# Axial attention as one run of 32 interleaved units, with the next queries and a projection inside it

## The chip, the cores and the metric

The kernel runs on one core of a Trainium2 chip. The metric is the device time of one execution in microseconds (us), from its first to its last instruction and what lies around it. The median of three runs before the change is 3224.26 us (3221.07 to 3228.34).

## What is computed

A sequence of 512 tokens of width 1024 goes through two transformer blocks of a first kind (each once) and two layers of a second kind. Only the second kind is touched. In float32:

```python
def second_block(x, ...):
    for l in range(2):
        h = rmsnorm_2(x, norm_mix_pre[l])
        qa, ka, va, pu, qc, kc, vc, gl = split(h @ w_in[l])
        ya = global_axial_attention(qa, ka, va, qk_norm_q[l], qk_norm_k[l])
        yb = pool_mixer(pu, w_pool[l], pool_scale[l])
        yc = neighbourhood_attention(qc, kc, vc, rpb[l])
        merged = sum(sigmoid(gates) * branches(ya, yb, yc))
        x = x + rmsnorm_2(merged @ w_out[l], norm_mix_post[l])
        h = rmsnorm_2(x, norm_ffn_pre[l])
        x = x + rmsnorm_2(conv_gated_mlp(h, ...), norm_ffn_post[l])

def global_axial_attention(q, k, v, gq, gk):
    # 8 query heads, 2 key/value heads, head width 64, no mask
    q = rope_2d(rmsnorm(q, gq), row, col) * 64 ** -0.5
    k = rope_2d(rmsnorm(k, gk), row, col)
    o = softmax(q @ k.T) @ v
```

The neighbourhood attention has eight heads with keys and values of their own and a bias and a mask for each pair of tokens.

## The kernel before, in words

Activations lie transposed, channels on partitions. A projection multiplies split operands: each weight tile and each activation has a high and a low part, and `three` (L470 to L472) issues three matmuls for each of the eight 128-channel steps k. One such step is called a part below. Weights come in entries: SyncE loads an entry into `raw` (L339), GpSimd splits it into `wh` and `wl` (L449 to L452) once TensorE is through with the buffer, and TensorE waits for `w_split`. There are two buffers, used in turn.

An attention works in units: one head and one tile of 128 queries against all 512 keys. TensorE computes the scores into bank S0 or S1, VectorE scales or biases them and takes the row's minimum (`score`, L1400 in the axial stage, L1404 elsewhere; scores are kept negated), ScalarE takes the exponential and its sum (`soften`, L1106), TensorE transposes the result with four matmuls (`transposed`, L621), ScalarE copies it from PSUM (`copy_turned`, L1112), and TensorE multiplies by the values. These steps of different units overlap: in slot t TensorE issues the scores of unit t, the transposes of unit t - 2 and the weighted matmuls of unit t - 3. Every engine runs its instructions in the order written and waits on counting semaphores.

The **axial stage** of a layer (`axial` in each engine's block, `attend` and `units`) has four groups of eight units, each with two query heads, one for each key head. Groups 0 to 2 are the iterations of a loop, group 3 stands behind it. The probabilities are stationary in the weighted matmuls and the values move, 64 columns (`weighted`, L627). VectorE scales each unit's output into `y_tok` (L1433); at a group's end four matmuls transpose it (L615), ScalarE and VectorE split it into `yh` and `yl` (L1117, L1415). Into slots 0 to 2 of a group go the eight parts of the next group's query projection (`AHEAD`, `q_part`, result in bank PA). Its result is scaled (`scale_q`, L1589) and squared (`q_square`, L1165), copied with a gain (L1170), summed by head on TensorE (`q_sum`, L774), rooted on ScalarE (`q_root`, L1178, a function of another table than the exponential) and rotated: TensorE permutes the channels (`turn_rotate`, L782), VectorE multiplies by cosine (`q_cosine`, L1574) and sine and adds (`turn`, L1579, L1582). `TURN` gives the slots; the sine product waits until slot 9, since the turned queries overwrite `q_sb`, which the group's own scores still read.

Behind the stage TensorE runs the neighbourhood's first query and key projection (`qk_part(H("na_q0", l), 0, 2 * DT)`, 16 parts) and its value projection (`v_projection`, L566 to L568).

The **neighbourhood stage** (`attention` with kind "na") is one unrolled run of 32 units. Even slots issue two score matmuls, on partitions 0 to 63 and 64 to 127 (L683). The values are stationary, 64 columns, and the transposed probabilities move, so the two heads of a pair write the two halves of one bank (`weighted_pair`, L722). The softmax's division is done once for a group: TensorE spreads the reciprocals over a bank (`den_turn`, L737), ScalarE copies them (L1157), VectorE multiplies (`y_divide`, L1454). `FILL` says how many parts of the next group's projections go into each of a group's eight slots, `last_plan` those of the last twelve slots, `Y_TURN` where the divisions stand. The other attentions of the kernel use the same function.

## Time and profile before

| | |
|---|---|
| median of three runs | 3224.26 us |
| the profiled execution's own time | 3222.63 us |
| its span, first to last instruction | 3220.5 us |
| mean granted TensorE clock | 0.98 of 2.4 GHz |
| TensorE busy | 3101.5 us |
| GpSimd, VectorE, ScalarE busy | 1661.9, 1420.2, 796.3 us |

The profile is one execution on the chip. PE is TensorE's matmuls, PEld its weight loads, DVE is VectorE, ACT ScalarE, POOL GpSimd, SP SyncE. L470 is line 470 of the kernel. In a list of instructions in order of time (the timeline), a line has the start in us from the span's start, the duration, the engine, line, operation, out<-in, the number of records merged, and in brackets the engine's idle time before it and what ended it. Float32 matmuls leave two records each. Matmuls are pipelined, so their durations overlap; the steps from start to start are what they cost. A line of windows has the stretch in us from the span's start, its length, the busy time and (x) the instructions of PE, PEld, DVE, ACT and POOL, the mean granted clock (PEclk), the DMA engines' busy share and GB/s.

### The profile page before, as it was taken

The page shows a single profiled execution, that of the slowest core. Times are in us where ns is not written, and L with a number is a line of the kernel's source. Part 1 is how long each engine was busy: PE and PEld are TensorE (multiplying, and loading weights), DVE is VectorE, ACT ScalarE, POOL GpSimd, SP SyncE. Part 2 cuts the span into 40 slices and gives each one's busy share as a digit, 9 for nine tenths or more (in the row PEclk, how much of TensorE's full clock was granted, in tenths as well). Part 3 has the DMA queues.
Part 4 walks back from the last instruction along what each step waited for, and adds up shares of the span by engine and source line. Part 5 has one row for each costly group of instructions (what it writes and reads, how often), then busy time and mean ns, then how long its engine had stood idle before and what let it go on. Part 6 is the DMA issues. An engine that isn't in the chain of part 4 may idle for free.

```text
span 3220.5 us, 45047 instructions
## 1 busy us (share of the span) xinstructions
PE 3101.5 (96%) x14716; PEld 2438.9 (76%) x14716; DVE 1420.2 (44%) x2535; ACT 796.3 (25%) x1441; POOL 1661.9 (52%) x1254
## 2 busy tenths in 40 slices
PE   8998999999799999899999999999899999999998
PEld 6776888886578888667678878888667678878886
DVE  3244444223444431542533476631633434476622
ACT  2333221113322210243421122210242411132201
POOL 4334666663156667312346656676312356656674
PEclk9999999999999999999999999999899999999999
DMA  6251223322022233101412222232112322222232
GB/s 159 74 167 63 96 93 104 107 95 66 27 79 97 93 109 105 52 26 51 101 59 98 90 74 98 95 110 95 40 33 56 83 79 97 86 72 98 98 107 83
DMA packets 99595, 274.79 MB, mean 85 GB/s; under 512 B 38126, under 2 KB 38894, under 8 KB 99490
## 3 DMA queue, kind: packets, MB, share of 16 engines
q1 hardware_dynamic: 97328, 269.07, 25.9%
q10 hardware_dynamic: 2162, 4.36, 0.7%
q8 instruction: 61, 1.00, 0.1%
q14 instruction: 44, 0.36, 0.0%
HBM read 269.66 MB, written 11.54 MB: 87 GB/s over the span
## 4 chain that ended last, share of the span: by engine, by line
PE 71%; DVE 3%; issue 2%; ACT 1%; DVEq 0%; ACTq 0%
PE PA L470 11%; PE PA L471 10%; PE PA L472 10%; PE PB L470 8%; PE PB L471 8%; PE PB L472 8%; PE T L621 2%; PE O L627 2%; PE S L590 2%; PE O L722 1%; PE S L683 1%; PE O L502 1%; DVE strip L1756 0%; DVE tmps L1365 0%; DVE hl L1326 0%
## 5 line engine op out<-in xcount | busy, mean ns | idle before, releaser
L452 POOL TENSOR_TENSOR wl<-raw,wh 128x1024 fp32r<-128x1024 f32 (+2 forms) x416 | 1129.2, 2714 | 33.3
L449 POOL TENSOR_TENSOR zero<-zero 128x1 f32<-128x1 f32 x416 | 82.4, 198 | 1494.0 <-PE PA L472 786.9
L470 PE MATMUL PA<-hh,wh 128*128 128x512 f32 x1392 | 563.5, 405 | 27.9 <-DVE hl L1326 8.3
L471 PE MATMUL PA<-hl,wh 128*128 128x512 f32 x1392 | 548.9, 394 | 0.0
L472 PE MATMUL PA<-hh,wl 128*128 128x512 f32 x1392 | 548.4, 394 | 0.0
L450 POOL CAST wh<-raw 128x1024 fp32r<-128x1024 f32 (+2 forms) x416 | 476.3, 1145 | 0.0
L470 PEld LDWEIGHTS PA<-hh,wh 128*128 128x128 f32 x1392 | 265.4, 191 | 136.4 <-issue 66.0
L470 PE MATMUL PB<-hh,wh 128*128 128x512 f32 x896 | 357.1, 399 | 0.0
L472 PE MATMUL PB<-hh,wl 128*128 128x512 f32 x896 | 349.3, 390 | 0.0
L471 PE MATMUL PB<-hl,wh 128*128 128x512 f32 x896 | 349.1, 390 | 0.0
L472 PEld LDWEIGHTS PA<-hh,wl 128*128 128x128 f32 x1392 | 265.4, 191 | 57.4
L471 PEld LDWEIGHTS PA<-hl,wh 128*128 128x128 f32 x1392 | 265.2, 191 | 53.0 <-issue 1.6
L1106 ACT ACTIVATE probs<-biased,stats 128x512 f32<-128x512 f32 (+2 forms) x240 | 155.2, 647 | 406.7 <-PE T L621 222.0
L1685 DVE SCALAR_TENSOR_TENSOR tmps<-S,cols,tmps 128x511 f32<-128x511 f32 (+1 forms) x264 | 197.9, 750 | 39.6 <-DVE tmps L1685 19.8
L470 PEld LDWEIGHTS PB<-hh,wh 128*128 128x128 f32 x896 | 168.2, 188 | 47.5 <-issue 14.4
L472 PEld LDWEIGHTS PB<-hh,wl 128*128 128x128 f32 x896 | 168.1, 188 | 35.6
L471 PEld LDWEIGHTS PB<-hl,wh 128*128 128x128 f32 x896 | 168.6, 188 | 33.8 <-issue 1.2
L621 PEld LDWEIGHTS T<-ident,probs 128*128 128x128 f32 x792 | 98.0, 147 | 72.0 <-issue 36.8
L1202 ACT ACTIVATE T<-tmps 128x512 f32<-128x512 f32 x88 | 53.0, 602 | 391.9 <-DVE tmps L1685 391.9
L470 PE MATMUL PA<-acth,wh 128*128 128x512 f32 x352 | 137.4, 390 | 0.0
L471 PE MATMUL PA<-actl,wh 128*128 128x512 f32 x352 | 137.0, 389 | 0.0
L472 PE MATMUL PA<-acth,wl 128*128 128x512 f32 x352 | 136.9, 389 | 0.0
(298 smaller groups left out, 4865.6 us busy)
## 6 DMA issues: line engine op xcount, KB each, us to landing
raw<-in_w_up SPq DMA_DIRECT2D x176, 512.0 KB, 3.4
raw<-in_w_down SPq DMA_DIRECT2D x64, 768.0 KB, 4.2
raw<-in_w_merge SPq DMA_DIRECT2D x48, 768.0 KB, 4.1
raw<-in_w_out SPq DMA_DIRECT2D x32, 512.0 KB, 3.4
strips_na<-in_rpb SPq DMA_DIRECT2D x1, 7620.0 KB, 31.7
raw<-in_w_pool SPq DMA_DIRECT2D x12, 512.0 KB, 3.4
raw<-in_w_na_qk SPq DMA_DIRECT2D x12, 512.0 KB, 3.4
raw<-in_w_na_v SPq DMA_DIRECT2D x8, 512.0 KB, 3.4
```

Source lines behind the costliest of these rows:

```text
L449: nc.gpsimd.tensor_tensor(zero[:, :], zero[:, :], zero[:, :], ALU.add)
L450: nc.gpsimd.tensor_copy(wh[s][:, 0:width], raw[s][:, 0:width]).then_inc(w_head, 1)
L452: nc.gpsimd.tensor_tensor(wl[s][:, 0:width], raw[s][:, 0:width], wh[s][:, 0:width].bitcast(F), ALU.subtract).then_inc(w_split, 1)
L470: mm(dst, h_, rh, start=first, stop=False)
L471: mm(dst, h_, rl, start=False, stop=False)
L472: return mm(dst, l_, rh, start=False, stop=last)
L590: mm(SB[t % 2][:, 0:L], q_sb[r, qt * P:qt * P + P], k_sb[r, 0:L], start=True, stop=True).then_inc(s_ready, 1)
L621: last = nc.tensor.transpose(TB[t % 2][:, k * P:k * P + P], probs[t % 2][:, k * P:k * P + P], ident[:, :])
L627: last = mm(OB[t % 2][:, 0:dv], probsT[t % 2][:, k * P:k * P + P], values(k), start=(k == 0), stop=(k == L // P - 1))
L1106: A(probs[t % 2][:, 0:L], biased[t % 2][:, 0:L], ACT.Exp, scale=-1.0, bias=mn[:, t % 8:t % 8 + 1], accum_out=den[:, t % 8:t % 8 + 1]).then ...
L1202: A(GELU[:, :], tmp[0][:, :], f).then_inc(gelu_ready, 1)
L1685: ins = STT(out=dst[:, lo:hi], in0=src[:, lo - d:hi - d], scalar=w(k), in1=dst[:, lo:hi], op0=ALU.mult, op1=ALU.add)
```

## The change

The axial stage becomes a third kind of `attention`, unrolled over 32 units in the neighbourhood's form: scores in pairs, values stationary, division once a group at slots 11, 19, 27 and 35. Keys lie in `kr_sb`, values in `tmp[4]`; the queries of successive groups alternate between `q_sb` and `qr_sb`. The next queries' projection parts keep slots 0 to 2 of a group. The whole turn now lies within the group: scaled in slot 3, squared in 4, the sums and the permutation on TensorE in slot 5 (`q_turn`, the permutation into PA instead of PB), the sine product in place in PSUM and the sum in slot 6 (`q_turned`), the root on ScalarE in slot 6, its reciprocal in slot 7. The 16 parts of the neighbourhood's first projection move from behind the stage into slots 24 to 34.

```diff
-        c.update(a=3, b=8, u=32, g=4, d=4 * (UNIT_LINKS[kind] + TURN_LINKS), r=4)
+        c.update(a=3, b=2 + 3, u=32, g=4, d=TURN_LINKS + UNIT_LINKS[kind], r=4, dr=16, dc=4)
...
-UNIT_LINKS = {"causal": 0, "na": 2, "diff": 8 + 4 + 1 + 3, "axial": 8, "mla": 4 + 1}
+UNIT_LINKS = {"causal": 0, "na": 2, "diff": 8 + 4 + 1 + 3, "axial": 3 * 3, "mla": 4 + 1}
...
-AHEAD = {"axial": [3, 3, 2, 0, 0, 0, 0, 0, 0, 0, 0, 0]}
...
-FILL = [3, 3, 2, 2, 3, 3, 0, 0]
+FILL = {"moba": [3, 3, 2, 2, 3, 3, 0, 0], "axial": [3, 3, 2, 0, 0, 0, 0, 0]}
+FILL["diff"] = FILL["dil"] = FILL["na"] = FILL["moba"]
 Q_AT, K_AT = 3, 6
 Y_TURN = {"moba": (15, 23, 27, 35), "diff": (15, 23, 30, 38)}
+Y_TURN["axial"] = (11, 19, 27, 35)
...
-TURN = dict(scale=3, square=4, sum=5, root=5, cosine=6, rotate=7, turn=9)
+TURN = dict(scale=3, square=4, sum=5, cosine=5, turn=6, root=6, invert=7)
...
+def axial_turn(b, n):
+
+    return {**b, "e": b["e"] + 2 * (n - 1), "a": b["a"] + n - 1, "b": b["b"] + 2 + n - 1, "r": b["r"] + n, "turn": n}
...
-        rq = stats[:, 108:116]
+        rq_of = stats[:, 108:116], stats[:, 88:96]
...
+        turned_q, axial_key, axial_v = strip[0][:, 0:S], kr_sb, tmp[4]
...
                 pe.wait_ge(s_taken, b["u"] + 2)
                 pe.wait_ge(pt_copied, b["u"] + 2)
...
                 def part(j):
+                    if j == 0 and after_turns is not None:
+                        pe.wait_ge(ax_done, after_turns)
                     if j == DT:
...
-                full = kind == "na"
+                full = kind in ("na", "axial")
+                values = (lambda g, c, k: axial_v[:, k * P + c:k * P + c + 64]) if kind == "axial" else (
+                    lambda g, c, k: V[:, k, g * P + c:g * P + c + 64])
...
-                parts = sum((qk_parts({**b, **{n: b[n] + m * g for n, m in (("e", 2), ("a", 1), ("b", 1))}},
-                                      *((y_split, 2 * (b["g"] + max(g - 1, 0)) + 1) if kind == "diff" else
-                                        (den_copied, b["dc"] + max(g - 1, 0))))
-                             for g in range(3)), []) + list(last_parts)
-                slots = FILL * 3 + list(last_plan)
+                if kind == "axial":
+                    parts = sum((q_parts(axial_turn(b, n)) for n in (1, 2, 3)), []) + list(last_parts)
+                else:
+                    parts = sum((qk_parts({**b, **{n: b[n] + m * g for n, m in (("e", 2), ("a", 1), ("b", 1))}},
+                                          *((y_split, 2 * (b["g"] + max(g - 1, 0)) + 1) if kind == "diff" else
+                                            (den_copied, b["dc"] + max(g - 1, 0))))
+                                 for g in range(3)), []) + list(last_parts)
+                slots = FILL[kind] * 3 + list(last_plan)
                 slots += [0] * (end + 1 - len(slots))
                 assert sum(slots) == len(parts)
...
                 def score(t):
                     g, head, qt = t // 8, t % 2, t // 2 % 4
-                    if t == 0:
+                    if kind == "axial":
+                        if t % 8 == 0:
+                            pe.wait_ge(ax_done, b["r"] + g + 1)
+                    elif t == 0:
                         pe.wait_ge(pa_taken, b0["a"] + 2)
                         pe.wait_ge(pb_taken, b0["b"] + 2)
                     elif t % 8 == 0:
...
-                    mm(SB[head][:, 0:span(t)], queries[g % 2][r, qt * P:qt * P + P], keys[g % 2][r, 0:span(t)],
+                    mm(SB[head][:, 0:span(t)], queries[g % 2][r, qt * P:qt * P + P],
+                       (axial_key if kind == "axial" else keys[g % 2])[r, 0:span(t)],
                        start=True, stop=True).then_inc(s_ready, 1)
...
                     if t in turns:
-                        (y_turn if kind == "diff" else den_turn)(b, turns.index(t))
+                        (y_turn if kind == "diff" else den_turn)(b, turns.index(t), kind)
+                    if kind == "axial" and t < 24 and t % 8 == TURN["sum"]:
+                        q_turn(axial_turn(b, t // 8 + 1))
                     for part in parts[sum(slots[:t]):sum(slots[:t + 1])]:
                         part()
...
-                            weighted_pair(OB[g % 2], tv // 2 % 4, span(tv), g)
-
-            def weighted_pair(bank, qt, L, g):
+                            weighted_pair(OB[g % 2], tv // 2 % 4, span(tv), lambda head, k: values(g, 64 * head, k))
+
+            def weighted_pair(bank, qt, L, values):
...
-                        c = g * P + head * 64
-                        last = mm(bank[r, q], V[:, k, c:c + 64], probsT[head][:, k * P:k * P + P], start=(k == 0),
+                        last = mm(bank[r, q], values(head, k), probsT[head][:, k * P:k * P + P], start=(k == 0),
                                   stop=(k == L // P - 1))
...
-                if g < 3:
+                if g < 3 and kind == "axial":
+                    pe.wait_ge(pb_taken, b["b"] + 2 + min(g + 1, 3) + 1)
...
+            def q_parts(b):
+
+                def part(k):
+                    if k == 0:
+                        pe.wait_ge(ax_done, b["r"])
+                    q_part(b, k, k + 1)
+
+                return [lambda k=k: part(k) for k in range(DT)]
+
+            def q_turn(b):
+
+                pe.wait_ge(den_copied, b["dc"] + b["turn"] - 1)
+                q_sum(b["b"], b["r"])
+                pe.wait_ge(ax_n, b["r"] + 1)
+                mm(PA[:, :], perm[1][:, :], turned_q, start=True, stop=True).then_inc(ax_rot, 1)
+
...
-                def group(i, ahead):
-                    bi = step(b, i, **STEP["axial"])
-                    pe.wait_ge(ax_done, bi["r"] + 1)
-
-                    attend(bi, 8, "axial", lambda h, k: tmp[4][:, k * P + h * 64:k * P + h * 64 + 64], 64,
-                           ahead=step(b, i + 1, **STEP["axial"]) if ahead else None, plan=AHEAD["axial"])
-
-                with pe.Fori(0, 3) as i:
-                    group(i, True)
-                group(3, False)
+                mm(PB[:, :], perm[1][:, :], src, start=True, stop=True).then_inc(ax_rot, 1)
...
-                axial_kv(H("axial_kv", l)); pool_tiles(H("pool", l), H("axial_kv", l), H("axial", l)); axial(H("axial", l))
-                qk_part(H("na_q0", l), 0, 2 * DT)
-                v_projection(H("na_v", l), True)
+                axial_kv(H("axial_kv", l)); pool_tiles(H("pool", l), H("axial_kv", l), H("axial", l));
+                q0 = H("na_q0", l)
+                attention(H("axial", l), None, "axial", qk_parts(q0, den_copied, q0["dc"] - 1, after_turns=q0["r"]),
+                          [2, 2, 2, 1, 1, 0, 0, 2, 2, 2, 2])
+                v_projection(H("na_v", l))
...
+                    if kind == "axial" and t < 24:
+                        bn = axial_turn(b, t // 8 + 1)
+                        if t % 8 == TURN["square"]:
+                            q_square(bn["a"] + 2, gain)
+                        if t % 8 == TURN["root"]:
+                            q_root(bn["r"])
...
-                A(qr_sb[:, :], tmp[2][:, :], ACT.Copy, scale=gain).then_inc(ax_n, 1)
+                A(turned_q, tmp[2][:, :], ACT.Copy, scale=gain).then_inc(ax_n, 1)
...
-                    at = 2 * (t % 4) + t // 4
-                    TS(biased[t % 2][:, 0:L], SB[t % 2][:, 0:L], rq[:, at:at + 1], None, ALU.mult, ALU.min,
+                    rq = rq_of[t // 8 % 2]
+                    TS(biased[t % 2][:, 0:L], SB[t % 2][:, 0:L], rq[:, c:c + 1], None, ALU.mult, ALU.min,
...
-                        c = 0 if dv == P else 64 * (tv // 4)
-                        TS(y_tok[0][:, tv % 4, c:c + dv], OB[tv % 2][:, 0:dv], rden[:, tv:tv + 1], None,
-                           ALU.mult).then_inc(o_taken, 1)
-                    if ahead is not None:
-                        if t == TURN["scale"]:
-                            scale_q(ahead)
-                        elif t == TURN["cosine"]:
-                            q_cosine(ahead["r"])
-                        elif t == TURN["turn"]:
-                            link(v.reciprocal(rq, rq_root))
-                            turn(-0.125, ahead["b"], ahead["r"], q_sb[:, :])
...
+                chain_at(b["d"] + (TURN_LINKS if kind == "axial" else 0))
+                if kind == "na":
...
+                    if kind == "axial" and t < 24:
+                        bn = axial_turn(b, g + 1)
+                        if t % 8 == TURN["scale"]:
+                            scale_q(bn)
+                        if t % 8 == TURN["cosine"]:
+                            q_cosine(bn["r"])
+                        if t % 8 == TURN["turn"]:
+                            q_turned(bn)
+                        if t % 8 == TURN["invert"]:
+                            dve.wait_ge(pb_taken, bn["b"] + 2)
+                            link(v.reciprocal(rq_of[(g + 1) % 2], rq_root))
+                    elif t < 24 and t % 8 == Q_AT:
                         take_q(ahead(g), g + 1)
-                    if t < 24 and t % 8 == K_AT:
+                    if kind != "axial" and t < 24 and t % 8 == K_AT:
                         take_k(ahead(g), g + 1)
...
+            def q_turned(b):
+
+                dve.wait_ge(ax_rot, b["r"] + 1)
+                link(STT(out=PA[:, :], in0=PA[:, :], scalar=-0.125, in1=rope[:, 1, :], op0=ALU.mult, op1=ALU.mult))
+                TT(queries[b["turn"] % 2][:, :], tmp[0][:, :], PA[:, :], ALU.add).then_inc(ax_done, 1)
...
-                axial(H("axial", l), l)
-                q0 = H("na_q0", l)
-                dve.wait_ge(s_ready, q0["u"] + 1)
-                take_q(q0, 0); take_k(q0, 0); v_copy(H("na_v", l))
+                attention(H("axial", l), "axial", 0, H("na_q0", l))
+                v_copy(H("na_v", l))
```

## Rows read from the trace of the kernel before

**Rows 1.** The page, busy time of each engine

```profile
PE 3101.5 (96%) x14716; PEld 2438.9 (76%) x14716; DVE 1420.2 (44%) x2535; ACT 796.3 (25%) x1441; POOL 1661.9 (52%) x1254
```

**Rows 2.** Windows, first layer: four axial groups, first projection, neighbourhood stage

```profile
1376.93:1411.24 34.31, 32.98 (x151) 21.65 (x151) 11.62 (x37) 15.88 (x31) 4.03 (x6) 0.86 0.06 16
1411.24:1441.06 29.82, 28.55 (x151) 19.18 (x151) 12.38 (x39) 16.34 (x33) 4.02 (x6) 1.00 0.10 35
1441.06:1476.40 35.34, 34.74 (x152) 23.52 (x151) 12.39 (x39) 16.52 (x33) 7.07 (x6) 0.81 0.09 30
1476.40:1497.63 21.23, 20.43 (x117) 13.57 (x117) 9.66 (x34) 10.96 (x26) 0.00 (x0) 1.00 0.00 1
1497.63:1508.40 10.77, 10.77 (x51) 8.92 (x50) 1.45 (x3) 0.66 (x2) 3.57 (x3) 1.00 0.02 3
1530.47:1631.10 100.63, 99.39 (x693) 69.08 (x692) 47.08 (x135) 46.77 (x103) 29.36 (x22) 1.00 0.32 80
```

**Rows 3.** Windows of the second layer: third axial group; sum of the five stretches

```profile
2396.60:2431.88 35.28, 34.68 (x151) 23.41 (x150) 12.38 (x39) 16.46 (x33) 7.08 (x6) 0.81 0.09 30
...
sum 135.77, PE 132.51 PEld 90.17 DVE 47.51 ACT 60.47 POOL 18.71; mean PE 26.50 PEld 18.03 DVE 9.50 ACT 12.09 POOL 3.74
```

**Rows 4.** Timeline of TensorE, fourth axial group

```profile
1487.71 1.12 PE L590 MATMUL S<-k_sb,q_sb 64*128 64x512 f32 x2
...
1490.19 1.12 PE L590 MATMUL S<-k_sb,q_sb 64*128 64x512 f32 x2
```

**Rows 5.** Timeline of TensorE, neighbourhood stage

```profile
1543.31 0.50 PE L470 MATMUL PB<-hh,wh 128*128 128x512 f32 x1
...
1545.49 0.60 PE L621 MATMUL T<-ident,probs 128*128 128x128 f32 x4
...
1549.76 1.13 PE L683 MATMUL S<-k_sb,q_sb 64*128 64x512 f32 x4
...
1551.40 1.09 PE L722 MATMUL O<-probsT,V 128*64 128x128 f32 x16
1552.43 0.66 PE L621 MATMUL T<-ident,probs 128*128 128x128 f32 x4
1553.02 1.13 PE L683 MATMUL S<-kr_sb,qr_sb 64*128 64x512 f32 x4
...
1576.76 1.05 PE L737 MATMUL PB<-ident,stats 128*64 128x128 f32 x16
1577.73 0.66 PE L621 MATMUL T<-ident,probs 128*128 128x128 f32 x4
```

**Rows 6.** Timeline of GpSimd, a split behind the first projection

```profile
1510.12 2.40 POOL L452 TENSOR_TENSOR wl<-raw,wh 128x1024 fp32r<-128x1024 f32 x1
```

**Rows 7.** Timeline of all engines, the turn of the next queries, first axial group

```profile
1395.10 0.62 ACT L1165 ACTIVATE tmps<-tmps 128x512 f32<-128x512 f32 x1
...
1395.62 0.71 ACT L1170 ACTIVATE qr_sb<-tmps,cols 128x512 f32<-128x512 f32 x1
...
1395.77 1.05 PE L774 MATMUL PB<-onesblk,tmps 128*128 128x2 f32 x8 [0.22 <-ACT tmps L1165]
...
1397.42 0.72 ACT L1106 ACTIVATE probs<-biased,stats 128x512 f32<-128x512 f32 x1 [1.09 <-PE T L621]
...
1398.14 0.58 ACT L1112 ACTIVATE probsT<-T 128x512 f32<-128x512 f32 x1
...
1398.73 1.28 ACT L1178 ACT_TABLE_LOAD   x1
...
1399.25 0.75 DVE L1400 TENSOR_SCALAR_CACHE_REDUCE biased<-S,stats 128x512 f32<-128x512 f32 x1 [2.50 <-PE S L590]
...
1400.03 0.27 ACT L1178 ACTIVATE stats<-PB,eps 128x8 f32<-128x8 f32 x1
```

**Rows 8.** Timeline of TensorE, start of the first axial group

```profile
1376.93 2.06 PE L590 MATMUL S<-k_sb,q_sb 64*128 64x512 f32 x2 [1.76 <-DVE q_sb L1582]
...
1383.01 1.12 PE L590 MATMUL S<-k_sb,q_sb 64*128 64x512 f32 x2
```

More of the change, by code:

```diff
@@ L1178, in q_root @@
                 A(rq_root, PB[:, 0:8], ACT.Sqrt, scale=1.0 / 64, bias=eps[:, 0:1]).then_inc(pb_taken, 1)
-            def axial(b, gain):
-                b = after_first(b)
-                with act.Fori(0, 3) as i:
-                    units({**step(b, i, **STEP["axial"]), "gain": gain}, 8, "axial", i, ahead=step(b, i + 1, **STEP["axial"]))
-                units(step(b, 3, **STEP["axial"]), 8, "axial", 3)
             def mla(b):
@@ L1279, in _ @@
                 q_root(ax["r"])
-                axial(ax, gain)
+                attention(ax, "axial", 0, gain=gain)
                 attention(H("na", l), "na", 8)
@@ L1556, in attention @@
                             in1=yh[:, ytile + g, :].bitcast(F), op0=ALU.mult, op1=ALU.subtract).then_inc(y_split, 2)
-                done(4 * UNIT_LINKS.get(kind, UNIT_LINKS["causal"]))
+                done((1 if kind == "axial" else 4) * UNIT_LINKS.get(kind, UNIT_LINKS["causal"]))
             def done(per):
```

104 lines of the change are left out of this document (33 added, 71 removed).

## The prediction

> **What bounds the kernel now.** I read the page first: TensorE is busy for 3101.5 of the span's 3220.5 us [rows 1], so only what shortens TensorE's own queue, or its few stalls, can move the time. Next I cut the part that the diff touches into windows by group, from a group's first score matmul to the next group's [rows 2, 3]. The reader is to see three things. In the first layer the four axial groups take 34.31, 29.82, 35.34 and 21.23 us and the neighbourhood's first projection behind them 10.77: 131.47 together. In the second layer the same five stretches sum to 135.77. And TensorE is busy in 95% or more of nearly all of them, so the stage is bound by TensorE's instructions, not by waits; the third group is 5.5 us longer than the second for the same work, with a mean granted clock of 0.81 instead of 1.00, that is partly at 1.2 GHz instead of 2.4.
>
> Then the timeline, for what a unit (one head, one query tile) costs. In the axial stage without projection work between, one score matmul, four transposes and four weighted matmuls repeat every 2.48 us (1487.71 to 1490.19) [rows 4]. The neighbourhood stage, which already has the form that the change gives to the axial one, runs a pair of units every 3.26 us (1549.76 to 1553.02), 1.63 a unit [rows 5]. Its two score matmuls, on the upper and lower 64 rows, take 1.13 us together, as one does in the axial stage (1.12), and its weighted matmuls, with values stationary and 64 columns each, 1.03 us for both heads. With 0.59 for a unit's transposes (1552.43 to 1553.02), twice, a score pair's own step is what is left of 3.26, about 1.06. That halving is the gain to expect.
>
> **The change part by part**, per layer, steps taken start to start.
>
> *Units.* 32 units become 16 pairs: 16 x 3.26 = 52.2 us [rows 5].
>
> *Projection parts.* Three parts (nine matmuls) take 1543.31 to 1545.49, 2.18 us, so 0.73 each with the hand-over [rows 5]. The 24 parts for the next queries stay, 16 of the neighbourhood's first projection come in from behind the stage: 40 x 0.73 = 29.2. With those 16 go all that they issue: their two weight entries are loaded and split earlier (the buffers come free at the third group's parts, long before slot 24), and VectorE's two copies of their result sit at slots 29 and 36. These moves cost nothing: in the windows before, GpSimd is busy 4.03 to 7.07 us of 30, VectorE about 12 [rows 2]. If that cover were gone, TensorE would wait for a split at the v projection. That is the one close place: its second entry's buffer comes free in slot 34, a cast and a split end some 3.6 us later (2.40 of it the split [rows 6]), and the projection wants it only after the rest of slot 34, the last turn and its first entry, over 5 us later. SyncE's loads for the neighbourhood's bias strips stand behind these entries and keep their place relative to the v projection.
>
> *Turns.* Dividing a group by its sums is now one matmul group of 1576.76 to 1577.73, 0.97, four times: 3.9 [rows 5]. It replaces four y transposes a group, with their drain at each group's end, and takes the 32 small VectorE scalings away. The query turn keeps its two TensorE steps, the sums (1.05 long, 0.95 step) and a 512-column permutation matmul, which I take as a score, 1.06 [rows 5, 7]: 3 x 2.0 = 6.0.
>
> Work: 52.2 + 29.2 + 3.9 + 6.0 = 91.3.
>
> *Check of this way of adding.* The neighbourhood stage has 16 pairs, 60 parts, four turns: 52.2 + 43.8 + 3.9 = 99.9, against 100.63 measured [rows 2]. So 0.7 is left for start and tail; I add it here too.
>
> *Start.* The first score and three parts run at 1.2 GHz: 1376.93 to 1383.01 is 6.1 us [rows 8] instead of 1.06 + 2.18. That stays: +2.8.
>
> *New waits.* These I walk with the engines' orders, from the issue of score pair (4, 5) of a group as zero. TensorE: pair to 1.06, transposes of unit 2 to 1.65, weighted pair to 2.65, then the query turn in slot 5. It waits for ScalarE, whose order is: exp of unit 4 (score pair 1.15, VectorE 0.8, so 1.97 to 2.69), copy of unit 2 (to 3.3), square (0.52, to 3.8), gain copy (0.71, to 4.5) [rows 7]. The sums therefore start at 3.95, a wait of 1.3. Behind the waiting instruction stand the permutation, unit 3's transposes and slot 6's scores; these transposes end at 6.6, and exp 5 waits for them: 6.7 to 7.4, copy 3 to 8.0, exp 6 8.6 to 9.3, copy 4 to 9.9. Now the root with its table load, 1.28 + 0.27, a copy of 0.6, and in slot 7 the load back for exp, 1.28 [rows 7]: exp 7 ends at 14.1, copy 5 at 14.7. TensorE's slots 6 and 7 (6.6 to 9.85) get what they need; the next group's score pair waits for VectorE's score 7, which stands behind the turned queries (two operations of 0.7 from 8.5) and ends at 10.7: a wait of 0.95. Its eight parts (5.8 us) let ScalarE catch up but for 0.25 in front of weighted pair (4, 5), which wants copy 5. VectorE waits in slot 7 for the root (11.5) and for ScalarE's copy (12.1), and holds up score 8; but TensorE wants what comes of score 8 only in slot 2. So 2.5 us in each of three groups: 7.5. Bounds for this term: nothing, if the turn's inputs come in time, and 4.1 a group, if all that ScalarE does for the turn (0.52 + 0.71 + 1.28 + 0.27 + 1.28) fell on TensorE. I take the walk, which lies between and uses the order that the code gives.
>
> The Trainium skill speaks against this cover. "ScalarE: Activation LUTs", section "What ACT_TABLE_LOAD costs", adds a drain of about 1.38 us to each load's 1.28. The trace disagrees: a copy starts at 1398.14 for 0.58, the load at 1398.73, and the root at 1400.03, 0.02 us behind the load [rows 7]. I leave the drain out of the sum; by the page, two loads at each of six turns would add 6 x 2.76, an estimate of 16.6 us.
>
> *Stage after:* 91.3 + 2.8 + 7.5 + 0.7 = 102.3 us. Gain: 131.47 - 102.3 = 29.2 in the first layer, 135.77 - 102.3 = 33.5 in the second, **62.7** together. In the second layer more is gained since low-clock stretches go.
>
> The profiled execution took 3222.63 us, 2.13 over its span; the median of the runs is 3224.26, 1.63 above it. 3222.63 - 62.7 = 3159.9; on the median's footing **3161.6**.
>
> **Rivals.**
>
> *The clock stays low in places.* The third group lost 5.5 us in each layer at a mean of 0.81 [rows 2, 3]. For: slots 3 to 7 have no projection parts, and the turn brings a wait and matmuls of two columns. Against: units now follow more densely, and the neighbourhood stage ran at 1.00 throughout [rows 2]. One such stretch a layer: + 11, 3173; one at each of the six turns: + 33, 3195.
>
> *ScalarE is later than walked.* Per pair it has 2 x (0.72 + 0.58) = 2.6 us against TensorE's 3.26 [rows 5, 7], so a delay at the turn is worked off only by 0.66 a pair until the parts come. If each of the turn's two loads held it up twice as long as its 1.28 [rows 7], TensorE would wait 2.6 us more at each of six turns: + 15, 3177. The page "TensorEngine Tiling (Array Packing)", section "PSUM Bottleneck", of the Trainium skill warns of just this: tiling speeds TensorE but not the copies out of PSUM.
>
> *The turn hides wholly.* ScalarE is early enough: - 15, so 3147. Against it is the order in slot 4, where exp 4 must come first.
>
> *The halves don't overlap here*, so that the change doesn't do what it says: a pair pays 1.06 and 1.03 twice: 16 x 2.1 x 2 = 67 given back, 3229. Against: same shapes and row halves as [rows 5]; only the tensors of keys and values differ.
>
> *Slower: the whole stage at 1.2 GHz.* Place: the axial stage, if its waits kept the lower level from the start (a score takes 2.06 us there [rows 8] against 1.12 [rows 4]), since the group boundaries with long matmul runs are gone. Price: 91.3 us of work doubled, less the 2.8 and 7.5 that it absorbs, + 81 a layer: 3324. It ends slower than before once 125 us of the two stages run low, since half of that, 62.7 us, is then lost. Against: the windows before recover at every set of parts.
>
> **How the numbers follow.** Forecast 0.55 (own range 3151 to 3171: a wait per turn between 0.7 and 4.1), clock 0.20, ScalarE later 0.08, turn hidden 0.12, no overlap 0.03, whole stage low 0.02. The range reaches from the hidden turn, 3146, past ScalarE late and most of the clock case, to 3185. Only the last two cases end within 0.2% (6.4 us; about what a measurement of this kernel can tell from no change) or slower: faster 0.95, same 0.02, slower 0.03.
>
> **What would show it.** Right: S pairs of 1.13 in the axial stage and 3.26 between pairs in slots without parts; projection and attention together about 102 us in both layers; a wait for ScalarE's square before L774 of about 1.3 and one before slot 0's scores of about 1; granted clock 1.00 from the second group on; the v projection starting at once; the neighbourhood stage still 100.6. Wrong: a clock below 0.9 in any group after the first; waits at the turn above 4 us; a wait for a split at the v projection; a stage above 112 us.

## The result, and the profile after

The changed kernel takes 3168.8 us (median of 4 runs, 3165.1 to 3169.2) against 3224.2 for the kernel before, measured beside it: ratio 0.9825, 95% interval 0.9813 to 0.9838. It is faster by 55.4 us. The forecast was 3161.6, so it was too low by 7.2 us. The range, the direction and the mechanism of the gain held; the waits and the clock were taken too low. The profiled execution took 3168.89 us with a span of 3167.1.

First the page of the profile, busy time of each engine, against [rows 1]:

```profile
PE 3039.9 (96%) x14812; PEld 2395.7 (76%) x14812; DVE 1400.9 (44%) x2439; ACT 795.7 (25%) x1437; POOL 1658.1 (52%) x1254
```

TensorE is busy 61.6 us less; its span shrank by 53.4. So some 8 us went into new idle time. To see where, the windows of the two stages, cut as in [rows 2, 3] from a group's first score matmul to the next. The neighbourhood's first projection now lies inside the fourth group. First layer, and behind it the neighbourhood stage (columns: window, length, then busy time of PE, PEld, DVE, ACT, POOL, granted clock, DMA share, GB/s):

```profile
1379.39:1401.64 22.25, 20.36 (x107) 12.88 (x107) 8.05 (x21) 10.38 (x22) 4.02 (x6) 0.87 0.09 24
1401.64:1426.24 24.60, 22.11 (x163) 14.91 (x163) 9.70 (x27) 15.29 (x31) 4.03 (x6) 1.00 0.14 44
1426.24:1452.93 26.69, 23.82 (x162) 15.49 (x163) 10.30 (x28) 15.70 (x32) 7.06 (x6) 0.94 0.12 40
1452.93:1484.19 31.26, 30.02 (x232) 21.42 (x233) 10.28 (x30) 17.52 (x36) 5.20 (x6) 1.00 0.06 18
...
1506.17:1607.00 100.83, 99.36 (x693) 69.09 (x692) 46.55 (x135) 46.76 (x103) 29.57 (x23) 1.00 0.32 80
```

Second layer:

```profile
2301.53:2323.53 22.00, 20.11 (x107) 12.67 (x107) 8.05 (x21) 10.38 (x22) 4.02 (x6) 0.88 0.08 25
2323.53:2349.56 26.03, 23.60 (x162) 15.40 (x162) 10.03 (x27) 15.16 (x31) 4.03 (x6) 0.93 0.12 41
2349.56:2377.74 28.18, 24.85 (x163) 16.48 (x163) 9.96 (x28) 15.82 (x32) 7.06 (x6) 0.88 0.12 38
2377.74:2409.02 31.28, 30.03 (x232) 21.42 (x232) 10.29 (x30) 17.53 (x36) 5.19 (x6) 1.00 0.06 18
```

The stage with the projection takes 104.8 us (131.47 before) and 107.5 us (135.77 before): 26.7 and 28.3 us gained, 102.3 forecast for each. The neighbourhood stage is unchanged (100.83 against 100.63). Outside the two stages the profiled executions differ by 1.6 us: the first stage begins 2.4 us later with nothing of the change ahead of it, the stretch between the stages is shorter by the same 2.4, and what follows the second stage takes 1.5 longer.

The table of waits of TensorE, first layer:

```profile
PE PB L778 <- ACT y_tok L1151: 4.9, 2, 2.4
PE O L708 <- ACT probsT L1104: 2.2, 4, 1.1
PE S L667 <- DVE q_sb L1569: 1.8, 1, 1.8
PE PB L778 <- ACT tmps L1159: 1.2, 1, 1.2
```

The third row is the stage's start and was there before [rows 8]. The others are new. L778 is the first matmul of the turn of the queries, and it waits for two different things. The last row is the one forecast, ScalarE's square, 1.2 us, but only once: in the first turn. The other two turns wait 2.43 us for ScalarE's copy L1151, the copy of the division's spread. The timeline of ScalarE ahead of the second turn shows why:

```profile
1417.26 0.72 ACT L1098 ACTIVATE probs<-biased,stats 128x512 f32<-128x512 f32 x1 [0.49 <-DVE biased L1388]
...
1418.14 0.60 ACT L1104 ACTIVATE probsT<-T 128x512 f32<-128x512 f32 x1
1418.63 0.62 ACT L1159 ACTIVATE tmps<-tmps 128x512 f32<-128x512 f32 x1
1419.15 0.71 ACT L1164 ACTIVATE strip<-tmps,cols 128x512 f32<-128x512 f32 x1
1419.76 0.59 ACT L1151 ACTIVATE y_tok<-PB 128x512 f32<-128x512 f32 x1
```

Exponential, copy, square, gain copy and, last, the division copy, which ends at 1420.35. TensorE's turn starts behind it, at 1420.47. The sums are written into PB, the bank in which the division's spread of the group before still stands, and `q_turn` begins with a wait for `den_copied`. The square had ended at 1419.25, 1.1 us before the copy. The first turn has no division before it, hence its shorter wait.

The third turn, in TensorE's timeline:

```profile
1442.00 1.09 PE L708 MATMUL O<-probsT,tmps 128*64 128x128 f32 x16
1445.53 1.05 PE L778 MATMUL PB<-onesblk,tmps 128*128 128x2 f32 x8 [2.43 <-ACT y_tok L1151]
1446.44 1.68 PE L765 MATMUL PA<-strip,perm 128*128 128x512 f32 x2
1447.91 1.06 PE L595 MATMUL T<-ident,probs 128*128 128x128 f32 x4
1448.90 1.77 PE L667 MATMUL S<-kr_sb,q_sb 64*128 64x512 f32 x4
1450.61 0.66 PE L595 MATMUL T<-ident,probs 128*128 128x128 f32 x4
```

Behind the wait the permutation takes 1.68 and a score pair 1.77 us, which at full clock take 1.10 and 1.13. Windows over the stretches behind the four 2.43 us waits (at 1420.47, 1445.53, 2342.37 and 2368.96):

```profile
1421.00:1425.00 4.00, 4.00 (x29) 2.38 (x30) 1.46 (x4) 1.49 (x4) 0.00 (x0) 1.00 0.00 0
1446.40:1450.60 4.20, 4.20 (x12) 1.70 (x11) 0.12 (x1) 1.30 (x3) 0.00 (x0) 0.59 0.00 0
2343.00:2348.00 5.00, 5.00 (x20) 2.33 (x19) 1.37 (x4) 1.30 (x3) 0.00 (x0) 0.66 0.00 0
2369.00:2375.00 6.00, 6.00 (x18) 3.55 (x18) 0.76 (x2) 1.30 (x3) 0.00 (x0) 0.50 0.00 0
```

Three of the four run wholly or mostly at 1.2 GHz. TensorE is busy all through these windows, so length times what is missing from a clock of 1.00 is the time lost: 1.7 us in the first layer and 1.7 + 3.0 = 4.7 in the second.

So the theory to test: the whole shortfall hangs on ScalarE's order in slots 3 and 4. Rivals: ScalarE's work as a whole is too much, so that a wait only moves; the table loads hold it up; the low clock comes from elsewhere.

### The profile page after: what moved, and what is told of

It reads as the page before. It is cut to its first block, busy times and chain, and to the rows that moved or that the text cites. A ratio compares the mean times of both kernels' runs of the same rounds, so it can differ in the third digit from the quotient of the medians.

```text
span 3167.1 us, 44727 instructions
## 1 busy us (share of the span) xinstructions
PE 3039.9 (96%) x14812; PEld 2395.7 (76%) x14812; DVE 1400.9 (44%) x2439; ACT 795.7 (25%) x1437; POOL 1658.1 (52%) x1254
## 4 chain that ended last, share of the span: by engine, by line
PE 70%; DVE 3%; ACT 2%; issue 2%; DVEq 0%; ACTq 0%
PE PA L461 11%; PE PA L463 10%; PE PA L462 10%; PE PB L461 9%; PE PB L462 8%; PE PB L463 8%; PE O L708 2%; PE S L667 2%; PE T L595 2%; PE O L493 1%; DVE hl L1314 1%; DVE tmps L1353 0%; PE PB L725 0%; DVE strip L1741 0%; PE O L601 0%
## 5 line engine op out<-in xcount | busy, mean ns | idle before, releaser
L1192 ACT ACTIVATE acth<-T 128x512 f32 x88 | 52.7, 599 | 336.7 <-DVE T L1697 336.7
```

## The experiments

All are edits of the changed kernel. The unedited one was timed in another session than these, so I compare ratios to the kernel before, and stages by their windows.

**ScalarE copies the division ahead of the square, in slot 4.**

```diff
+            def den_early(b, turns, t):
+                if t - 1 in turns:
+                    g = turns.index(t - 1)
+                    act.wait_ge(yt_ready, 2 * (b["g"] + g) + 3)
+                    act.wait_ge(y_split, 2 * (b["g"] + max(g - 1, 0)) + 1)
+                    A(flat_y(g), (PB if g < 3 else O0)[:, :], ACT.Copy).then_inc(den_copied, 1)
...
+                    if kind == "axial":
+                        den_early(b, turns, t)
                     if kind == "axial" and t < 24:
                         bn = axial_turn(b, t // 8 + 1)
                         if t % 8 == TURN["square"]:
                             q_square(bn["a"] + 2, gain)
...
-                    if t - 1 in turns:
+                    if kind != "axial" and t - 1 in turns:
```

> The changed kernel took 3168.8 us; its axial stage with the projection 104.8 us in the first layer and 107.5 in the second. Edit: in slot 4 ScalarE copies the division before it squares the queries (the order was square, gain copy, division copy). Theory A (the turn of the queries waits for the division copy, because the sums share its bank, and that copy stands last): the wait before the turn's first matmul in turns 2 and 3 of each layer goes from 2.43 us to about 1.8 and is now ended by the square, not the copy; but the gain copy ends at 2.43 as before and the permutation behind the sums wants it, so that only about 0.3 to 0.6 us a turn come off, four times: 1 to 2.5 us of 3168.8; the first turn of each layer (1.23) stays. Rival B (the copy is only the last of several that come together, what is late is ScalarE as a whole): the wait stays at 2.4 under another name, time within 1 us.

Measured: 3165.5 us, ratio 0.9812 (0.9799 to 0.9826). Stages 101.8 and 105.5. The waits before the turn in the first layer:

```profile
PE PB L778 <- ACT tmps L1168: 4.7, 3, 1.7
```

All three turns now wait for the square (L1168 here), 1.74 in the later two (1.8 expected). So the division copy was what had ended the wait. The stages are shorter by 3.0 and 2.0 us; the waits account for 1.4 in each, and in the first layer the low stretch of the third group is gone (clock 1.00, 24.35 us). In the second it moved to the second group (0.87, 27.06 us). The intervals of the ratio overlap with the unedited kernel's, so the 3.3 us in the time are not shown by it alone.

**TensorE's turn behind the transposes of its slot.**

```diff
-                    if kind == "axial" and t < 24 and t % 8 == TURN["sum"]:
-                        q_turn(axial_turn(b, t // 8 + 1))
                     for part in parts[sum(slots[:t]):sum(slots[:t + 1])]:
...
                             weighted_pair(OB[g % 2], tv // 2 % 4, span(tv), lambda head, k: values(g, 64 * head, k))
+                    if kind == "axial" and t < 24 and t % 8 == TURN["sum"]:
+                        q_turn(axial_turn(b, t // 8 + 1))
```

> Edit: in slot 5 TensorE issues the turn of the queries (sums and permutation) behind the slot's transposes and no longer ahead of them; ScalarE's order stays. Theory A (what stands behind the waiting instruction costs more than the wait: unit 3's transposes, on which exp 5 and copy 3 hang): the transposes' 0.6 us now fill the wait, so that turns 2 and 3 wait about 1.8 and the first turn 0.6, and ScalarE's chain behind them starts 3 us earlier, so that the waits before the weighted matmuls (0.38 and 1.06 us before) and before the next group's scores shrink: 0.6 to 1.5 us a turn, six turns, 3168.8 - (4 to 9) = 3160 to 3165. Rival B (the waits are total ScalarE work, so that any order gives the same): within 1.5 us of 3168.8, the wait reappears in slots 6 to 8. Rival C: the clock falls again behind the turn and takes the gain back, granted clock below 0.90 in the group after a turn.

Measured: 3163.0 us, ratio 0.9807 (0.9794 to 0.9821); stages 103.5 and 103.3. The waits at the turn shrink by the transposes' 0.6 (1.84 and 0.6), as Theory A says, but those before the weighted matmuls grow, against it, from 2.2 to 2.9 in the first layer and from 2.7 to 2.8 in the second:

```profile
PE PB L778 <- ACT y_tok L1151: 3.7, 2, 1.8
PE O L708 <- ACT probsT L1104: 2.9, 4, 1.8
```

Part of what is taken from one wait comes back in the next, since ScalarE's chain did not get earlier. The third group still has a clock of 0.93 in both layers. The interval overlaps with the unedited kernel's here too, so that the gain rests on the stages, 1.3 and 4.2 us shorter.

**ScalarE squares before the exponential of slot 3, and copies the division before that of slot 4.**

```diff
+                    if kind == "axial" and t < 24 and t % 8 == 3:
+                        q_square(axial_turn(b, t // 8 + 1)["a"] + 2, gain)
+                    if kind == "axial":
+                        den_early(b, turns, t)
                     if t < 32:
                         soften(u, t, S if full else (t // 2 % 4 + 1) * P)
...
-                        if t % 8 == TURN["square"]:
-                            q_square(bn["a"] + 2, gain)
```

The function `den_early` and the last part of the first experiment's edit are in it as well.

> Edit: ScalarE squares the queries before the exponential of slot 3 (not behind slot 4's copy) and copies the division before the exponential of slot 4; TensorE's order stays. Theory A (ScalarE's order in slot 4 is the whole of the turn's wait): the waits of 2.43 us (four) and 1.2 (two), 12 us in all, go down to 0.5 or less each, and the slots at 1.2 GHz behind them with them: about 8 to 14 us less, 3155 to 3161; stages about 100 us each. Rival B (the wait only moves: exp 3 and exp 4 are later by the square, the gain copy and the division copy, 1.9 us, and the transposes of slots 4 and 5 wait instead): new waits before the transposes or the weighted matmuls of 1 us and more in slots 4 to 6, time 3165 or above.

Measured: **3153.4 us**, ratio 0.9773 (0.9759 to 0.9786), clear of the unedited kernel's interval and 1.6 us below the lower end of Theory A's 3155 to 3161. The windows of the second layer:

```profile
2295.82:2317.66 21.84, 20.05 (x107) 12.71 (x107) 8.01 (x21) 10.38 (x22) 4.04 (x6) 0.87 0.08 25
2317.66:2339.87 22.21, 22.11 (x163) 14.93 (x163) 9.58 (x27) 15.06 (x31) 4.02 (x6) 1.00 0.15 48
2339.87:2362.52 22.65, 22.20 (x163) 14.95 (x163) 10.19 (x28) 15.46 (x32) 7.06 (x6) 1.00 0.16 47
2362.52:2393.57 31.05, 29.99 (x232) 21.43 (x233) 10.27 (x30) 17.62 (x36) 5.19 (x6) 1.00 0.05 18
```

Its waits, both rows of the table in either layer:

```profile
PE O L708 <- ACT probsT L1104: 3.1, 3, 1.7
PE S L667 <- DVE q_sb L1578: 1.8, 1, 1.8
```

No turn waits any more, and from the second group on the clock is 1.00 in both layers. The stages take 98.2 and 97.8 us, 6.6 and 9.7 less. ScalarE had as much work as before (58.5 us a layer against 58.9), so Rival B, that the wait only moves, holds for 0.9 us (2.2 to 3.1) of the first layer's 6.1. It holds in one place, the first group. The changed kernel waited there twice:

```profile
1393.55 1.09 PE L708 MATMUL O<-probsT,tmps 128*64 128x128 f32 x16 [0.56 <-ACT probsT L1104]
1395.87 1.05 PE L778 MATMUL PB<-onesblk,tmps 128*128 128x2 f32 x8 [1.23 <-ACT tmps L1159]
```

The edited one waits once, nearly as long:

```profile
1395.63 1.09 PE L708 MATMUL O<-probsT,tmps 128*64 128x128 f32 x16 [1.69 <-ACT probsT L1104]
```

There the early square and gain copy stand ahead of the exponential of unit 3 and of the copy that this pair wants. So the order of ScalarE's instructions explains the miss: the two long waits of a layer are gone, and with them the low clock of the middle groups.

**Both edits together.**

> Edit: both, ScalarE's early square and division copy and TensorE's turn behind the slot's transposes. Theory A: no wait above 0.3 us at any turn and nothing late behind it; the stage is then its work, 91.3 us, plus 2.8 for the slow start, 0.7 for start and tail and what the table loads leave (0 to 1 us a turn): 95 to 98 us a layer, 3168.8 - (7 to 12) - (10 to 12) = 3145 to 3152. Rival B (the waits move to the start of slots 3 to 5, or into the next group's first scores, where ScalarE's two table loads of 1.28 us fall): no better than either edit alone, 3157 to 3163. Rival C (the low clock does not come from these waits): waits gone, but groups with a granted clock of 0.87 to 0.94 as now, 3155 or above.

Measured: 3153.6 us, ratio 0.9775 (0.9762 to 0.9789); stages 98.0 and 96.7, the same 3.1 us before the weighted matmuls. My number (3145 to 3152) was missed: once ScalarE is early there is no wait left for the transposes to fill. What is left stands elsewhere: 1.69 us in slot 4 of the first group, as before, and 0.38 and 1.07 in slot 0 of the third and fourth.

**The root and its table loads in slot 5**, where this ScalarE is idle, on top of the early square and copy:

```diff
-TURN = dict(scale=3, square=4, sum=5, cosine=5, turn=6, root=6, invert=7)
+TURN = dict(scale=3, square=4, sum=5, cosine=5, turn=6, root=5, invert=7)
```

> Edit: as e3_scalar_early (3153.4 us, stages 98.2 and 97.8 us), and ScalarE takes the root with its two table loads in slot 5 instead of slot 6, where e3's ScalarE stands idle for 2 us ahead of the exponential of unit 6. Theory A (the 3.1 us of waits before the weighted matmuls that e3 leaves in each layer are the two table loads of slot 6, late): they go down to 1 us or less, 2 us a layer: 3148 to 3151; stages about 96. Rival B (the loads then delay exp 6, and TensorE waits at the group's end instead): the wait moves to slot 8's scores or transposes, 3152 to 3156.

Measured: **3149.3 us**, ratio 0.9764 (0.9750 to 0.9777); stages 96.7 and 96.5. The waits before the weighted matmuls go from 3.1 to 2.0 a layer, not below 1. The waits of 0.36 and 1.04 in slot 0 of the third and fourth group have shrunk to one of 0.29, so these were the loads; the 1.69 of the first group is unchanged and had nothing to do with them. Theory A took all three for the loads. Stages and median are in the expected places even so. The ratio's interval overlaps with that of the version before it, so the gain over that is read from the windows (1.5 and 1.3 us) and not from the times.

**Also the turned queries at the end of VectorE's slot 5**, no longer between its units 6 and 7:

```diff
-                        if t % 8 == TURN["turn"]:
-                            q_turned(bn)
...
                     if kind != "diff" and t - 4 in turns:
                         y_rest(b, ytile, turns.index(t - 4))
+                    if kind == "axial" and t < 24 and t % 8 == 5:
+                        q_turned(bn)
```

> Edit: as e9_root5, and VectorE adds up the turned queries at the end of slot 5 instead of between units 6 and 7. Theory A (the second score matmul of the next group's first pair waits 0.65 us for VectorE, which reads unit 7's scores only after the two operations of 0.7 us for the queries): this wait goes, 3 x 0.65 a layer, 4 us less than e9: 3144 to 3148; the first pair of a group takes 1.13 us instead of 1.72. Rival B (VectorE then waits in slot 5 for the permutation and reads unit 6 late by as much): no better than e9.

Measured: 3149.6 us, ratio 0.9765 (0.9750 to 0.9780); stages 95.7 and 95.9. The first pair of the third group, here and in the early-ScalarE version:

```profile
1423.27 1.13 PE L667 MATMUL S<-kr_sb,q_sb 64*128 64x512 f32 x4
```
```profile
1424.64 1.72 PE L667 MATMUL S<-kr_sb,q_sb 64*128 64x512 f32 x4
```

This part of Theory A holds: the wait of 0.6 for VectorE is gone. But 1.0 us of 1.8 a layer comes back before the weighted matmuls (2.0 to 3.0), in slot 0 of the third and fourth group, where TensorE now waits for ScalarE. The expected 3144 to 3148 was missed: the time is that of the version before, as Rival B says, though the wait comes back later than it says.

**The root left out.**

```diff
-                A(rq_root, PB[:, 0:8], ACT.Sqrt, scale=1.0 / 64, bias=eps[:, 0:1]).then_inc(pb_taken, 1)
+                A(rq_root, PB[:, 0:8], ACT.Copy, scale=1.0 / 64).then_inc(pb_taken, 1)
```

> Edit: the root in the turn of the queries is left out (ScalarE copies and scales the sums instead), so that slots 6 and 7 have no table loads: it leaves out part of the computation, the square root of the query norms. Theory A (the turn costs by ScalarE's order in slot 4, and the loads fall into slots that the next group's projection parts cover): only the wait before the next group's scores (0.7 us) and the weighted matmuls' (0.4 to 1.1) shrink: 1 to 2 us a turn, six turns, 3157 to 3164. Rival B (a load costs more than the 1.28 us that its row shows, by a drain of about as much again): 16 us and more less, below 3153. Rival C (wholly covered): within 2 us of 3168.8.

Measured: 3172.1 us, ratio 0.9839 (0.9822 to 0.9855). That is no gain, Rival C in kind, though 3.3 us above 3168.8 and not within 2; the intervals of the ratios overlap. ScalarE's busy time in the first stage falls by 8.2 us, from 58.9 to 50.7, the waits at the turn stay, and those before the weighted matmuls fall from 2.2 to 0.7:

```profile
PE PB L778 <- ACT y_tok L1151: 4.9, 2, 2.4
PE PB L778 <- ACT tmps L1159: 1.2, 1, 1.2
PE O L708 <- ACT probsT L1104: 0.7, 2, 0.6
```

The first stage is 1.7 us shorter; in the second (107.7) both middle groups run at 0.88, which takes the gain back. So eight microseconds of ScalarE's work a layer were hidden but for about 1.5, and the order of two instructions was worth more than all table loads.

About the drain of Rival B this time alone says little: the twelve loads' own 15.4 us did not show in it either. ScalarE's timeline in the changed kernel does, at the third group's start:

```profile
1428.40 1.28 ACT L1098 ACT_TABLE_LOAD   x1
1429.70 0.72 ACT L1098 ACTIVATE probs<-biased,stats 128x512 f32<-128x512 f32 x1
```

The exponential starts 0.02 us behind the end of the load that it needs, as the root did in [rows 7].

**Scores unpaired.**

```diff
-                    if t < 32 and t % 2 == 0:
+                    if t < 32 and kind == "axial":
+                        score(t)
+                    elif t < 32 and t % 2 == 0:
                         score(t); score(t + 1)
```

> Edit: in the axial stage TensorE issues each unit's score matmul in its own slot instead of two together; everything else stays, the weighted matmuls paired by column halves too. Theory A (two score matmuls on the upper and lower 64 rows run at the same time only if they stand next to each other, and this is half of the gain): a score costs its own step of 1.06, 16 more a layer: 17 us a layer, 34 in all, 3203; single scores of 1.1 us, 32 a layer. Since each step is then longer than ScalarE's work, the waits at the turns may shrink by up to 1 us each: 3197 to 3203. Rival B (the second score was hidden anyway behind waits for VectorE and ScalarE): below 3180.

Measured: 3198.1 us, ratio 0.9916 (0.9900 to 0.9933), as Theory A says; stages 122.6 and 120.4. In the timeline:

```profile
1418.28 1.12 PE L667 MATMUL S<-kr_sb,qr_sb 64*128 64x512 f32 x2
1419.33 1.09 PE L727 MATMUL PB<-ident,stats 128*64 128x128 f32 x16
```

A lone score takes 1.05 from start to start, as much as a pair. 32 of 1.05 are 34 us; 29 arrive, since the waits at the turns shrink (2.43 to 1.4 and 1.2 to 0.2), as expected, but low stretches come in: the first layer's second and third group run at 0.89 and 0.87. So issuing the scores in pairs is worth 29 of the change's 55.4 us.

**Weighted matmuls head by head.**

```diff
-                            weighted_pair(OB[g % 2], tv // 2 % 4, span(tv), lambda head, k: values(g, 64 * head, k))
-
-            def weighted_pair(bank, qt, L, values):
+                            weighted_pair(OB[g % 2], tv // 2 % 4, span(tv), lambda head, k: values(g, 64 * head, k),
+                                          kind == "axial")
+
+            def weighted_pair(bank, qt, L, values, by_head=False):
...
-                for k in range(L // P):
-                    for head in range(2):
+                order = [(k, head) for k in range(L // P) for head in range(2)]
+                for k, head in sorted(order, key=lambda kh: kh[1]) if by_head else order:
```

> Edit: in the axial stage the eight weighted matmuls of a pair go head by head (four of the one, four of the other) instead of alternating between the heads; same matmuls, same columns. Theory A (two matmuls into the two column halves of the array overlap only when they are neighbours): the pair's 1.03 us become about 2.1, 16 a layer, 34 us in all, 3199 to 3203. Rival B (with values stationary and 128 moving columns the matmuls are short against their weight loads, so that the order does not matter): within 5 us of 3168.8.

Measured: 3176.5 us, ratio 0.9854 (0.9838 to 0.9871); stages 111.1 and 111.2. Neither theory: 8 us, not 34. The timeline:

```profile
1459.68 1.58 PE L710 MATMUL O<-probsT,tmps 128*64 128x128 f32 x16 [1.06 <-ACT probsT L1106]
1461.19 0.50 PE L461 MATMUL PA<-hh,wh 128*128 128x512 f32 x1
```

A pair takes 1.51 us from start to start against 1.03 alternating: 0.48 more, not 1.03. 32 of them are 15 us; the waits at the turns give back some (2.43 to 1.9, 1.2 to 0.8). So alternating the heads is worth a third of the pair's time, not half. Why not half, no run here shows.

**The first projection back behind the stage.**

```diff
-                attention(H("axial", l), None, "axial", qk_parts(q0, den_copied, q0["dc"] - 1, after_turns=q0["r"]),
-                          [2, 2, 2, 1, 1, 0, 0, 2, 2, 2, 2])
+                attention(H("axial", l), None, "axial")
+                pe.wait_ge(ax_done, q0["r"])
+                pe.wait_ge(den_copied, q0["dc"] - 1)
+                qk_part(q0, 0, 2 * DT)
...
-                attention(H("axial", l), "axial", 0, H("na_q0", l))
-                v_copy(H("na_v", l))
+                attention(H("axial", l), "axial", 0)
+                take_q(H("na_q0", l), 0); take_k(H("na_q0", l), 0); v_copy(H("na_v", l))
```

> Edit: only the neighbourhood's first projection (16 parts) goes back behind the axial stage, where it was; the rest of the change stays. Theory A (its 16 parts cost 0.73 us each in either place, and the move hides only the stage's end, where TensorE otherwise waits for ScalarE and VectorE): the parts are worth 11.7 us inside and 10.8 behind, the stage's tail opens waits of 2 to 4 us in slots 29 to 35, and the neighbourhood's first scores wait for the copy of the projection: 1 to 3 us a layer more, 3171 to 3175. Rival B (the parts in slots 24 to 31 are what lets ScalarE catch up after the last turn and what brings the clock back): 5 us a layer and more, 3179 or above, and a granted clock below 0.9 in the last group. Rival C (the move brings nothing): within 1 us.

Measured: 3182.7 us, ratio 0.9869 (0.9853 to 0.9886): 13.9 us more, in Rival B's range. The windows of the last group with the projection behind it, both layers:

```profile
1453.80:1489.68 35.88, 31.28 (x233) 22.68 (x233) 11.01 (x31) 18.57 (x38) 3.57 (x3) 0.95 0.01 3
```
```profile
2388.12:2424.36 36.24, 31.18 (x234) 22.60 (x233) 10.68 (x31) 18.71 (x38) 3.57 (x3) 0.95 0.02 3
```

They take 4.6 and 5.0 us more, 9.6 of the 13.9. The waits before the weighted matmuls of this group rise in the first layer from 1.2 to 4.4 us, up to 2.5 at once: without parts between, ScalarE does not keep up with pairs. The rest of the time lies in the second layer's first two groups, which have no edit in them: they run at 0.74 and 0.88 and are 3.6 and 1.7 us longer, while the third is 1.7 shorter. Why the clock is lower there stays open. So Rival B is right that ScalarE catches up behind these parts, but its clock below 0.9 in the last group did not come (0.95), and the total lies in its range only by the low clock elsewhere.

## Why the prediction was right, and where it was off

**Units as pairs: right.** Score pairs of 1.13 us, weighted pairs of 1.09 as the neighbourhood stage had [rows 5], and undoing the pairing of the scores alone gave 29 us back. The rival that the halves don't overlap is refuted by that. Its price of 67 us was too high for the weighted half: head by head, the pairs cost 15 us more, not 33.

**Parts, weight loads, splits: right.** The parts lie inside for their own 0.73 each and no wait for a split appears; the v projection starts at once; the neighbourhood stage stays. What the prediction had at nothing, "These moves cost nothing", was a gain of its own: inside the stage these parts are the cover in which ScalarE catches up, 4.6 and 5.0 us in the two layers, by the experiment.

**The work terms: 2 us a layer too high.** The version with the turned queries in slot 5 has a stage of 95.7 us with 3.0 of new waits: 92.7 for work, start and tail, forecast 91.3 + 2.8 + 0.7 = 94.8. The turn is a part of it: from the sums to the next transposes it takes 0.91 + 0.95 = 1.86 us instead of 2.0, 0.4 a layer. Where the other 1.7 went the runs do not separate.

**The waits: the step that failed.** "The sums therefore start at 3.95, a wait of 1.3" took the square as the last thing the turn waits for. The walk through ScalarE stopped at the gain copy and never asked for `den_copied`, the first wait in `q_turn`, although the division copy stands behind the gain copy in the same slot. Measured are 1.2 in the first turn and 2.43 in the two others, 6.1 a layer instead of 3.9. Before the weighted matmuls 2.2 and 2.7 stand against 0.75 forecast; the second score of a group's first pair waits 0.6 (0.95 forecast, so this one was taken too high). Together 6.1 + 2.2 + 1.8 = 10.1 and 6.1 + 2.7 + 1.8 = 10.6, against 7.5.

**The clock: a rival that came true in part.** 92.7 + 10.1 = 102.8 leaves 2.0 us of the first stage's 104.8, and 92.7 + 10.6 = 103.3 leaves 4.2 of the second's 107.5. The low stretches above were worth 1.7 and 4.7, so the sum closes to within 0.5. The forecast had granted 1.00 from the second group on, and named "a clock below 0.9 in any group after the first" as a sign of being wrong. This sign came: the second layer's third group ran at 0.88. In all four versions without a wait at the turn the clock is 1.00 from the second group on in both layers; each of the seven with such waits, the unedited one among them, has one of these groups at 0.94 or less.

**The sum.** Per layer and against 102.3: work -2.1, waits +2.6 and +3.1, clock +2.0 and +4.2: 104.8 and 107.5. That is 7.7 for both layers, and 1.6 more came outside the stages: 9.3, against 9.0 between the profiled executions (3168.9, and 3159.9 forecast) and 7.2 between the medians. Part of the closeness is luck: waits and clock were 11.9 us off, and the work terms, too high by 4.2, hid a third of it.

**ScalarE's table loads: right to leave the drain out.** The forecast from [rows 7] was that 1.28 us is all a load takes, and the changed kernel's trace has the same 0.02 us behind a load. The Trainium skill states a drain of 1.38 us for each ("ScalarE: Activation LUTs", section "What ACT_TABLE_LOAD costs"), by which the twelve loads would add an estimate of 16.6 us; the traces disagree. The Trainium skill's warning in "TensorEngine Tiling (Array Packing)", section "PSUM Bottleneck", that the copies out of PSUM can become the limit, agrees in part with the waits before L708, which are for such a copy: 2.2 us in the first layer, and 4.4 in the one group that lost its parts. Of the 2.2, 1.5 go when the root and its loads are left out, so it is ScalarE's whole work that is late and not the copies alone.

**What the waits and the clock cost can be had back for the most part.** Over their 92.7 us the two stages of the changed kernel spend 26.9 us together. With the square, the division copy and the root moved in ScalarE's order 19.1 of them are gone (stages of 96.7 and 96.5), and the kernel takes 3149.3 us, 2.4% less than the kernel before and below the forecast.

## What to carry to other kernels

When a step moves into a pipelined slot, list every wait at its head, the one for the bank that it writes as well as those for its inputs, and walk the producing engine's order to the last of them. An instruction that another engine waits for goes first in its slot, ahead of work that has slack, but look at what it delays in turn: in the first group here the wait only moved. A wait can cost more than it says: in the second layer two waits of 2.43 us were followed by stretches at a low clock that cost 4.7 us more. Parts of dense work are also time in which a slower engine catches up: spread them where that engine is tightest.

## What was not expected

The same wait was followed by the low clock in some places and not in others: behind the 2.43 us wait at 1420.47 the windows above show 1.00, behind the one at 1445.53 they show 0.59. With all three turns of a layer waiting alike (1.74, 1.74 and about 1.2), the edited kernel of the first experiment had 1.00 throughout the middle groups of one layer and 0.87 in the second group of the other. Nor does it take a long wait. In the kernel before, the third group ran at 0.81 in both layers [rows 2, 3], and the three waits before the turn of the first layer were 0.2 us at most:

```profile
PE PB L774 <- ACT tmps L1165: 0.7, 3, 0.2
```

So removing the waits brought the clock back in this kernel, but what decides whether it falls behind a given turn, no run here shows.

The second surprise is that the weighted matmuls of two heads cost 1.51 us a pair one head after the other and 1.03 alternating, where their overlap was priced at half. The third is a stage that got 0.8 us shorter (96.6 to 95.8, means of both layers) without any change in the median, 3149.3 and 3149.6: at this size the windows tell more than the times, though each comes from one execution only.
